# Preparing the key exponents of a gated-linear-attention chunk on GpSimd instead of VectorE, in a one-core Trainium2 transformer kernel

## The chip, the cores and the metric

The kernel runs on one core of a Trainium2 chip. The metric is the time of one execution in microseconds of device time; the figure given for a kernel is the median of its runs. Less is better. The engines are called TensorE (PE, with its weight loads PEld), VectorE (DVE), ScalarE (ACT), GpSimd (POOL) and SyncE (SP).

## What is computed

The reference is two transformer blocks over 512 tokens of width 1024 with a context of 256 tokens: a block with retention, window and neighbourhood attention and a mixture of experts, and then a second block of two layers. Each layer of the second block has three branches (latent attention, pooling, gated linear attention). The change touches only the gated linear attention (GLA), which is run forward and backward over chunks of 128 tokens:

```python
def gla_scan(q, k, v, log_a, s0, with_out):
    ...
    def step(s, inp):
        qq, kk, vv, aa = inp
        b = jnp.cumsum(aa, axis=2)
        b_last = b[:, :, -1:, :]
        s_new = jnp.exp(b_last)[:, :, 0, :, None] * s + jnp.einsum('bhcd,bhce->bhde', kk * jnp.exp(b_last - b), vv)
        inter = jnp.einsum('bhcd,bhde->bhce', qq * jnp.exp(b), s)
        decay = jnp.exp(jnp.where(mask, b[:, :, :, None, :] - b[:, :, None, :, :], -jnp.inf))
        attn = jnp.einsum('bhid,bhjd,bhijd->bhij', qq, kk, decay)
        intra = jnp.einsum('bhij,bhje->bhie', attn, vv)
        return s_new, inter + intra
```

There are 4 heads with 64 key and 128 value features. The kernel computes `attn` without the five-index product: it cuts the 128 queries of a chunk into 4 segments of 32, takes the running sum `b` in the middle of a segment as `mid`, and uses exp(b - mid) for queries and exp(mid - b) for keys, both exponents held at or below a clamp.

## The kernel before

All activations lie feature-major in on-chip memory: 128 features on the partitions, tokens along the free axis. Every engine has its own instruction stream, written by hand in program order inside `program`, and streams wait for one another on counted semaphores. `E.sig(name)` raises a semaphore when an instruction is done, `E.next(name)` waits for its next value, `E.own()` waits for the last one that the engine itself raised. There is no planner; the order of the text is the order of the work. Products go to PSUM in numbered groups that rotate over three slots: `E.written(group)` waits until TensorE has written one, `E.taken(group)` until it has been read.

Weights stream through a ring of SyncE transfers. Most weight tiles are split into a high part (ScalarE, `high`, L1235) and a low part (GpSimd, `low`, L2175), one op of 1024 elements per partition each, for a three-product matmul. `low(n)` in the GpSimd stream does the next n tiles. Both parts have two buffers.

A layer of the second block (`for l in LAYERS` in each stream) has, up to the change: modulation and norm; projections for GLA queries, keys, values and gates; the running sums `gB` (VectorE, L1991); exponents of the state keys (L2000 to L2005), their exponential (ScalarE, L1468), product with the keys (L2011), 24 transposes (L560); state products `U` (TensorE) with the state scan (L2019, L2022). Then comes the **chunk loop**. Layer 0 does all six chunks of 128 tokens (`OWN_CHUNKS`), layer 1 only the four of the image, 2 to 5. Chunk buffers are double (`gChunk(c % 2)`): QI, QS (512 elements per partition each), KS (2048: 2 directions, 2 tiles, 4 segments, 128 keys) and QZ (1024). They overlay the buffers that the transposes and state products read, `gT1` and `gKT`. For one chunk c:

- VectorE `chunk_exponents(c)`: QS = b - mid (L2035), KS = mid - b for two directions (L2040, 1024 elements each), then the minimum with the clamp for QS (L2044) and KS (L2045);
- ScalarE `chunk_exps(c)`: exponentials of QS (L1477), KS (L1479) and of b into QI (L1480);
- VectorE `chunk_products(c)`: per direction QI times queries (L2053), QS times queries into the two halves of QZ (L2056), KS times keys (L2061);
- TensorE: scores `A` (32 matmuls of 128x64), then, after VectorE, the output `Y` (16 matmuls of 128x128 when a chunk is the first of a direction's scan, 24 otherwise);
- VectorE: masks of the scores out of PSUM (L2080, four of 256 elements), and the sum of the directions (L2085, 512), which releases `Y`;
- ScalarE: evacuation of `Y` (L1492).

VectorE runs `chunk_products(c)`, `chunk_exponents(c + 1)`, masks and sum of c, in this order, with `chunk_exponents` of the first chunk ahead of the loop. ScalarE runs `chunk_exps(c + 1)` before the evacuation of c. GpSimd has `low(17)` ahead of and across the loop and nothing else until the stage ends. All matmuls of the helper `mm` carry line L557, all transposes L560.

Of the kernel before, what the change touches and what calls it, by code (L numbers as in the profile page):

```python
# [19 lines left out]
P = 128  # L20
# [4 lines left out]
TT = TOK // P  # L25
# [10 lines left out]
CLAMP = 1280.0  # L36
# [181 lines left out]
def program(nc, dram, scratch, out):  # L218
# [7 lines left out]
    with ExitStack() as ctx:  # L226
        def sbuf(name, cols):
            return ctx.enter_context(nc.sbuf_tensor(name, [P, cols], f32))
# [10 lines left out]
        parts = parts.rearrange("p (s x n) -> p s x n", s=2, x=2)  # L239
        split_tiles = [n for n, name in enumerate(plan) if is_split(name)]  # L240
        split_reader = []
        par = sbuf("params_sb", NPAR)
        con = sbuf("consts_sb", NCONST)
        with nc.sbuf_tensor("arena", [P, ARENA], f32) as arena:
# [299 lines left out]
        def _(pe):  # L544
# [505 lines left out]
            for l in LAYERS:  # L1050
# [51 lines left out]
                for c in OWN_CHUNKS[l]:  # L1102
                    QI, QS, KS, QZ = gChunk(c % 2)
                    pe.wait_ge(*E.next("chunk_operands"))
                    ps = group("A", l, c)
                    for d in range(2):
                        for t in range(2):
                            for s in range(4):

                                at = ((2 * d + t) * 4 + s) * 64  # L1110
                                ins = mm(ps[:, at:at + 64], KS[:, d, t, s, :],
                                         QZ[:, 2 * d + t, s, :, :].rearrange("p b n -> p (b n)"), True, True)
                    ins.then_inc(psum_full, 1)
                    pe.wait_ge(*E.next("chunk_weights"))
                    ps = group("Y", l, c)
                    for h in range(4):
                        hp = 64 * (h % 2)
                        terms = [(gV[:, c, h * P:(h + 1) * P], gAT[:, h * P:(h + 1) * P])]
                        for d in range(2):
                            if c != SCAN[d][0]:  # L1120
                                terms.append((gS[hp:hp + 64, d, c, h // 2, :],
                                              QI[hp:hp + 64, 2 * d + h // 2, :]))
                        for n, (a, b) in enumerate(terms):
                            at = (h % 2) * 512 + (h // 2) * P
                            ins = mm(ps[:, at:at + P], a, b, n == 0, n == len(terms) - 1)
                    ins.then_inc(psum_full, 1)
# [80 lines left out]
        def _(act):  # L1207
# [221 lines left out]
            for l in LAYERS:  # L1429
# [44 lines left out]
                def chunk_exps(c):  # L1474
                    QI, QS, KS, _ = gChunk(c % 2)
                    act.wait_ge(*E.next("chunk_exponents"))
                    act_(QS, QS, ACT.Exp, scale=1.0 / 16)  # L1477
                    ks = KS.rearrange("p d t s n -> p (d t s n)")
                    act_(ks, ks, ACT.Exp, scale=1.0 / 16)  # L1479
                    act_(QI, gB[:, :, c * P:(c + 1) * P], ACT.Exp, scale=1.0 / 16)\  # L1480
                        .then_inc(*E.sig("chunk_decays"))
# [85 lines left out]
        def _(dve):  # L1567
# [392 lines left out]
            for l in LAYERS:  # L1960
# [67 lines left out]
                def chunk_exponents(c):  # L2028

                    QI, QS, KS, _ = gChunk(c % 2)  # L2030
                    b = gB[:, :, c * P:(c + 1) * P]
                    b4 = b.rearrange("p a (s n) -> p a s n", s=4)
                    mid = b4[:, :, :, 15:16]
                    dve.wait_ge(*E.own())
                    tt_(QS.rearrange("p a (s n) -> p a s n", s=4), b4, mid.to_broadcast([P, 4, 4, 32]),  # L2035
                        ALU.subtract)
                    for d in range(2):
                        E_in = mid[:, 2 * d:2 * d + 2, :, :].to_broadcast([P, 2, 4, P])
                        E_b = b[:, 2 * d:2 * d + 2, :].unsqueeze(2).to_broadcast([P, 2, 4, P])
                        ins = tt_(KS[:, d, :, :, :], E_in, E_b, ALU.subtract)  # L2040
                    ins.then_inc(*E.sig("dve_step"))
                    dve.wait_ge(*E.own())
                    q, k = QS.rearrange("p a n -> p (a n)"), KS.rearrange("p d t s n -> p (d t s n)")
                    V.tensor_scalar_min(q, q, CLAMP)  # L2044
                    V.tensor_scalar_min(k, k, CLAMP).then_inc(*E.sig("chunk_exponents"))  # L2045

                def chunk_products(c):
                    QI, QS, KS, QZ = gChunk(c % 2)
# [111 lines left out]
        def _(pool):  # L2160
# [68 lines left out]
            for l in LAYERS:  # L2229
                if l == 0:  # L2230
                    pool.wait_ge(*E.next("ctx2_loaded", 16))
                    pool.wait_ge(*E.next("residual_ready", 3 * KT))
                else:
                    pool.wait_ge(*E.own())
                pool.dma_start(scratch, R3).then_inc(sem("residual_saved"), 16)
                low(17)

                pool.wait_ge(*E.own())
                G_.memset(tick[:, 2:3], 0.0).then_inc(*E.sig("pool_stage_done"))
                pool.wait_ge(*E.next("act_stage_done"))  # L2240
                pool.wait_ge(*E.next("dve_stage_done"))
                pool.dma_start(area(MW, 1024), dram["t_mla"]).then_inc(sem("mla_tables_loaded"), 16)
                low(1)

                pool.wait_ge(*E.own())
                G_.memset(tick[:, 2:3], 0.0).then_inc(*E.sig("pool_stage_done"))
                pool.wait_ge(*E.next("act_stage_done"))
                pool.wait_ge(*E.next("dve_stage_done"))
                pool.dma_start(pCnt, dram["t_count"]).then_inc(sem("counts_loaded"), 16)
                for b in range(2):  # L2250
                    for c0, n in ((0, 8), (264, 16), (792, 8)):
                        ins = G_.memset(pX[:, b * (TOK + 32) + c0:b * (TOK + 32) + c0 + n], 0.0)
                if l == 1:
                    for b in range(2):
                        ins = G_.memset(pX[:, b * (TOK + 32) + 8:b * (TOK + 32) + 264], 0.0)
                ins.then_inc(*E.sig("pads_zero"))
                pool.wait_ge(*E.next("pads_zero"))
                pool.wait_ge(*E.next("counts_loaded", 16))
                low(4)
                for g in range(4):  # L2260
                    low()
                    pool.wait_ge(*E.taken("px", l, g))
                    u = pX[:, (g % 2) * (TOK + 32):(g % 2 + 1) * (TOK + 32)]
                    a, w = u, TOK + 32

                    lo = 0
                    for n in range(g + 1):
                        o = pS[:, (n % 2) * w:(n % 2 + 1) * w]
                        s1 = 1 if n == 0 else 2 ** (n - 1)
                        s2 = 0 if n == 0 else 2 ** (n - 1)  # L2270
                        new = lo + s1
                        G_.tensor_tensor(o[:, new:w - new], a[:, new - s1:w - new - s1],  # L2272
                                                a[:, new + s2:w - new + s2], ALU.add).then_inc(*E.sig("pool_step"))
                        pool.wait_ge(*E.own())
                        a, lo = o, new
                    segs = ([(8, 0, CTX)] if l == 0 else []) + [(280, CTX, SEQ)]
                    for x0, c0, n in segs:
                        ins = G_.tensor_tensor(pO[:, g, c0:c0 + n], a[:, x0:x0 + n], pCnt[:, g, c0:c0 + n],
                                               ALU.mult)
                    ins.then_inc(*E.sig("pool_step"))  # L2280
                    pool.wait_ge(*E.own())
                    for x0, c0, n in segs:
                        ins = G_.tensor_tensor(pO[:, g, c0:c0 + n], pO[:, g, c0:c0 + n], u[:, x0:x0 + n],
                                               ALU.subtract)
                    ins.then_inc(*E.sig("pooled"))
                    low()
                low(24 + 4 * len(parted(("l", l))))

                pool.wait_ge(*E.written("gate", ("l", l), 2, KT - 1))
                pool.wait_ge(*E.next("residual_saved", 16))  # L2290
                pool.dma_start(R3, scratch).then_inc(sem("residual_reloaded"), 16)
                low(6)
                pool.wait_ge(sem("residual_reloaded"), 16 * (l + 2))
                for k in range(KT):
                    pool.wait_ge(*E.next("update_ready"))
                    v = slice(0, TOK) if l == 0 else slice(CTX, TOK)
                    G_.tensor_tensor(R3[:, k, v], R3[:, k, v], mOUT[:, k, v], ALU.add)\
                        .then_inc(*E.sig("residual_updated"))
# [96 lines left out]
```

## Time and profile before

| | us |
|---|---|
| median of 3 runs | 3560.37 |
| lowest, highest | 3553.74, 3569.28 |
| profiled execution | 3560.11 |
| its span in the trace | 3558.3 |
| mean granted TensorE clock | 0.92 |

The profiled execution lies 0.3 us from the median, and 1.8 us of it are outside the span. The chunk loop of layer 0 runs from about 1801.6 to 1912 us of the span, that of layer 1 from about 2893.7 to 2974; together they are some 190 us, 5% of the span. A row of the timeline gives start, duration, engine, line, operation, output and inputs, shape and count, and in brackets how long the engine had been idle and who ended that. Durations of one instruction include time in which it has been issued and is held up.

### The profile page before, as it was taken

What the parts mean: (1) busy time and instruction counts of PE and PEld (TensorE: products, weight loads), DVE (VectorE), ACT (ScalarE), POOL (GpSimd) and SP (SyncE); (2) the same over time, 40 slices, a digit from 0 to 9 for tenths busy, and PEclk for the clock granted to TensorE, in tenths of its full rate; (3) what the DMA queues carried; (4) which work ended last, traced back from release to release, by engine and by line L of the source; (5) the groups of instructions that cost most, each with busy time, mean ns of one, the idle gap of its engine ahead of it and who ended that gap; (6) DMA issues with size and microseconds to landing.
All of it is one profiled execution on the core that took longest, in us unless ns stands there. A gap on an engine that the chain in (4) does not pass through costs nothing.

```text
span 3558.3 us, 35935 instructions
## 1 busy us (share of the span) xinstructions
PE 3106.5 (87%) x14810; PEld 2247.3 (63%) x14810; DVE 1066.0 (30%) x1387; ACT 847.8 (24%) x1223; POOL 662.6 (19%) x348
## 2 busy tenths in 40 slices
PE   6889899999869999987769699999997948799996
PEld 1656787788633333324657378999993746387885
DVE  1235512411341111122266543111115075542112
ACT  0422322322300000013322233211123222233222
POOL 0221320044200000001200001522222201006443
PEclk9899999999879999998857899999998967899998
DMA  9011210022239999984100001111124100002221
GB/s 390 36 48 42 43 60 12 14 98 99 87 132 358 383 369 362 372 330 159 48 1 26 28 1 54 60 60 60 68 88 188 59 12 30 24 7 100 100 97 71
DMA packets 56488, 406.87 MB, mean 114 GB/s; under 512 B 6352, under 2 KB 6352, under 8 KB 9760
## 3 DMA queue, kind: packets, MB, share of 16 engines
q1 hardware_dynamic: 52416, 375.41, 27.8%
q0 software_dynamic: 3936, 29.48, 2.4%
q8 instruction: 105, 1.72, 0.2%
q14 instruction: 31, 0.25, 0.0%
HBM read 396.48 MB, written 8.39 MB: 114 GB/s over the span
## 4 chain that ended last, share of the span: by engine, by line
PE 77%; DVE 10%; DMA 6%; ACT 4%; issue 1%; POOL 1%; SPq 0%; DVEq 0%; POOLq 0%; ACTq 0%
PE psum L557 73%; DMA ring<-in_weights 6%; PE psum L560 3%; DVE arena L1583 1%; DVE arena L1614 1%; DVE arena L1613 1%; ACT hidden_high L1256 1%; ACT hidden L1250 1%; DVE arena L1617 1%; POOL arena L2272 0%; DVE arena L2155 0%; DVE arena L1991 0%; DVE arena L2080 0%; DVE arena L2094 0%; ACT weight_parts L1235 0%
## 5 line engine op out<-in xcount | busy, mean ns | idle before, releaser
L557 PE MATMUL psum<-hidden_high,weight_parts 128*128 128x384 f32 (+1 forms) x3296 | 866.8, 364 | 56.2 <-DVE hidden_low L1596 41.8
L2175 POOL TENSOR_TENSOR weight_parts<-ring,weight_parts 128x1024 fp32r<-128x1024 f32 x218 | 532.1, 2442 | 1693.6 <-ACT weight_parts L1235 1688.2
L557 PE MATMUL psum<-arena 128*128 128x64 f32 (+8 forms) x2992 | 651.8, 372 | 92.7 <-DVE arena L2061 32.4
L557 PEld LDWEIGHTS psum<-hidden_high,weight_parts 128*128 128x128 f32 x3296 | 609.4, 191 | 132.5 <-issue 51.7
L557 PEld LDWEIGHTS psum<-arena 128*128 128x128 f32 (+3 forms) x2992 | 435.7, 214 | 249.9 <-issue 213.5
L557 PE MATMUL psum<-hidden_low,weight_parts 128*128 128x384 f32 (+1 forms) x1648 | 518.4, 362 | 0.0
L1235 ACT ACTIVATE weight_parts<-ring 128x1024 fp32r<-128x1024 f32 x218 | 231.0, 1061 | 1141.0 <-PE psum L557 1123.9
L557 PE MATMUL psum<-ring,arena 128*64 128x512 f32 (+1 forms) x1560 | 380.3, 604 | 44.5 <-DMA ring<-in_weights 39.3
L557 PE MATMUL psum<-arena_parts,weight_parts 128*128 128x512 f32 (+1 forms) x1728 | 368.5, 373 | 12.9 <-DVE arena_parts L1717 12.9
L557 PEld LDWEIGHTS psum<-arena_parts,weight_parts 128*128 128x128 f32 x1728 | 317.9, 190 | 58.4 <-issue 14.3
L1265 ACT ACTIVATE arena<-psum 128x512 f32<-128x512 f32 (+4 forms) x234 | 165.9, 713 | 696.5 <-PE psum L557 457.3
L557 PEld LDWEIGHTS psum<-hidden_low,weight_parts 128*128 128x128 f32 x1648 | 309.1, 192 | 26.6 <-issue 0.5
L557 PEld LDWEIGHTS psum<-ring,arena 128*64 128x64 f32 (+1 forms) x1560 | 105.5, 137 | 267.9 <-issue 162.8
L1704 DVE TENSOR_TENSOR arena<-arena,psum 128x512 f32<-128x512 f32 (+1 forms) x72 | 55.9, 777 | 595.1 <-PE psum L557 595.1
L1637 DVE TENSOR_REDUCE small<-psum 128x1 f32<-128x768 f32 (+3 forms) x144 | 122.9, 854 | 333.8 <-PE psum L557 333.8
L560 PE MATMUL psum<-consts_sb,arena 128*128 128x128 f32 x968 | 145.5, 286 | 64.3 <-DVE arena L2011 45.4
L557 PE MATMUL psum<-arena,consts_sb 128*128 128x512 f32 (+3 forms) x362 | 166.7, 596 | 29.5 <-DVE arena L1613 15.5
L560 PEld LDWEIGHTS psum<-consts_sb,arena 128*128 128x128 f32 x968 | 120.8, 149 | 87.9 <-DVE arena L2011 46.1
L1287 ACT ACTIVATE arena<-psum,small 128x768 f32<-128x768 f32 (+3 forms) x144 | 117.3, 815 | 225.1 <-DVE small L1637 222.9
L557 PE MATMUL psum<-arena,ring 128*128 128x384 f32 (+5 forms) x344 | 124.7, 529 | 31.0 <-DVE arena L2116 21.2
L557 PE MATMUL psum<-weight_parts,hidden_high 128*128 128x512 f32 (+1 forms) x480 | 139.2, 375 | 10.9 <-issue 8.8
L557 PEld LDWEIGHTS psum<-arena,consts_sb 128*128 128x128 f32 (+2 forms) x362 | 70.1, 201 | 110.8 <-issue 63.8
(224 smaller groups left out, 2039.1 us busy)
## 6 DMA issues: line engine op xcount, KB each, us to landing
ring<-in_weights SPq DMA_DIRECT2D x356, 1024.0 KB, 5.0
saved_residual<-residual POOLq DMA_DIRECT2D x2, 3072.0 KB, 14.3
residual<-saved_residual POOLq DMA_DIRECT2D x2, 3072.0 KB, 11.2
arena<-in_rpb POOLq DMA_DIRECT2D x16, 224.0 KB, 8.2
residual<-in_acts POOLq DMA_DIRECT2D x1, 3072.0 KB, 19.3
arena<-in_t_count POOLq DMA_DIRECT2D x2, 1536.0 KB, 7.4
residual<-in_acts POOLq DMA_DIRECT2D x1, 2048.0 KB, 11.0
out_x<-residual SPq DMA_DIRECT2D x8, 256.0 KB, 2.0
```

Of the source, the lines that this page charges most:

```text
L557: return nc.tensor.matmul(o, lhsT, rhs, start=start, stop=stop)
L560: return nc.tensor.transpose(o, a, C("ident")[0:a.shape[0], 0:a.shape[0]])
L1235: act_(parts[:, i % 2, 0, :], ring[:, at:at + 1024], ACT.Copy).then_inc(*E.sig("high_written"))
L1250: ins = act_(H3[:, k, CTX:TOK], H3[:, k, CTX:TOK], ACT.Identity, bias=mod[:, col + k, 0:1])
L1256: act_(Hhi[:, k, :], H3[:, k, :], ACT.Copy).then_inc(*E.sig("hidden_high"))
L1265: act_(dst, src, func, **kw).then_inc(*E.read(*name))
L1287: act_(pP[:, i % 2, 0:L + CTX], ps[:, 512 - L:768], ACT.Exp, bias=negmax[:, col:col + 1], accum_out=sums[:, col:col + 1]).then_inc(*E.read ...
L1583: V.reciprocal(r, r).then_inc(*E.sig("dve_step"))
L1613: tt_(tmp, ps[p0:p1, 0:SEQ], sin, ALU.mult).then_inc(*E.read("rot", *name))
L1637: ins = V.reduce_max(nm, ps[:, 512 - L:768], AXX, negate=True)
L1704: tt_(to, tok_view(mSG[:, gate_slot(f, b, g), :], chunks), bank_view(ps, chunks), ALU.mult).then_inc(*E.read("branch", key, b, g))
L2175: G_.tensor_tensor(parts[:, i % 2, 1, :], ring[:, at:at + 1024], parts[:, i % 2, 0, :], ALU.subtract).then_inc(*E.sig("tile_split"))
```

## The change

The key exponents (two subtractions and the minimum on KS) leave VectorE's `chunk_exponents` and are issued by GpSimd in a loop of its own over the layer's chunks. That loop stands after 12 of the 17 tile splits; the other 5 follow it. GpSimd first waits for both `decayed_keys` signals; for the first two chunks of a layer it then waits for the last state products of both directions to be written, and for every later chunk c until the scores of chunk c - 2 are written (`chunk_sums` records that group count in TensorE's stream). ScalarE waits for the new signal `key_chunk_exponents` between the exponential of QS and that of KS.

```diff
@@ TensorE, chunk loop, after the scores
                     ins.then_inc(psum_full, 1)
+                    chunk_sums.append(state["g"])
                     pe.wait_ge(*E.next("chunk_weights"))
@@ ScalarE, chunk_exps
                     act.wait_ge(*E.next("chunk_exponents"))
                     act_(QS, QS, ACT.Exp, scale=1.0 / 16)
+                    act.wait_ge(*E.next("key_chunk_exponents"))
                     ks = KS.rearrange("p d t s n -> p (d t s n)")
@@ VectorE, chunk_exponents
                     tt_(QS.rearrange("p a (s n) -> p a s n", s=4), b4, mid.to_broadcast([P, 4, 4, 32]),
-                        ALU.subtract)
-                    for d in range(2):
-                        E_in = mid[:, 2 * d:2 * d + 2, :, :].to_broadcast([P, 2, 4, P])
-                        E_b = b[:, 2 * d:2 * d + 2, :].unsqueeze(2).to_broadcast([P, 2, 4, P])
-                        ins = tt_(KS[:, d, :, :, :], E_in, E_b, ALU.subtract)
-                    ins.then_inc(*E.sig("dve_step"))
+                        ALU.subtract).then_inc(*E.sig("dve_step"))
                     dve.wait_ge(*E.own())
-                    q, k = QS.rearrange("p a n -> p (a n)"), KS.rearrange("p d t s n -> p (d t s n)")
-                    V.tensor_scalar_min(q, q, CLAMP)
-                    V.tensor_scalar_min(k, k, CLAMP).then_inc(*E.sig("chunk_exponents"))
+                    q = QS.rearrange("p a n -> p (a n)")
+                    V.tensor_scalar_min(q, q, CLAMP).then_inc(*E.sig("chunk_exponents"))
@@ GpSimd, layer of the second block
                 pool.dma_start(scratch, R3).then_inc(sem("residual_saved"), 16)
-                low(17)
+                low(12)
+                pool.wait_ge(*E.next("decayed_keys", 2))
+                for c in OWN_CHUNKS[l]:
+                    KS = gChunk(c % 2)[2]
+                    b = gB[:, :, c * P:(c + 1) * P]
+                    mid = b.rearrange("p a (s n) -> p a s n", s=4)[:, :, :, 15:16]
+                    n = (c if l == 0 else TT + c - 2) - 2
+                    if c >= OWN_CHUNKS[l][0] + 2:
+                        pool.wait_ge(psum_full, chunk_sums[n])
+                    else:
+                        for d in range(2):
+                            pool.wait_ge(*E.written("U", l, d, SCAN[d][-2]))
+                    for d in range(2):
+                        E_in = mid[:, 2 * d:2 * d + 2, :, :].to_broadcast([P, 2, 4, P])
+                        E_b = b[:, 2 * d:2 * d + 2, :].unsqueeze(2).to_broadcast([P, 2, 4, P])
+                        G_.tensor_tensor(KS[:, d, :, :, :], E_in, E_b, ALU.subtract).then_inc(*E.sig("pool_step"))
+                    pool.wait_ge(*E.own())
+                    k = KS.rearrange("p d t s n -> p (d t s n)")
+                    G_.tensor_scalar_min(k, k, CLAMP).then_inc(*E.sig("key_chunk_exponents"))
+                low(5)
```

## Rows read from the trace of the kernel before

**Rows 1.** The page: busy time by engine, and the chain that ended last.
```profile
PE 3106.5 (87%) x14810; PEld 2247.3 (63%) x14810; DVE 1066.0 (30%) x1387; ACT 847.8 (24%) x1223; POOL 662.6 (19%) x348
PE 77%; DVE 10%; DMA 6%; ACT 4%; issue 1%; POOL 1%; SPq 0%; DVEq 0%; POOLq 0%; ACTq 0%
```

**Rows 2.** Windows of layer 0's loop: length; busy PE, PEld, DVE, ACT, POOL; PEclk; DMA.
```profile
1798.00:1814.00 16.00, 0.03 (x2) 0.00 (x0) 12.28 (x20) 2.95 (x3) 0.00 (x0) 0.63 0.00 0
1822.00:1837.00 15.00, 12.87 (x48) 10.89 (x48) 11.17 (x19) 3.55 (x4) 0.00 (x0) 0.50 0.00 1
...
1852.00:1870.00 18.00, 14.58 (x56) 12.60 (x56) 12.46 (x22) 3.55 (x4) 0.00 (x0) 0.50 0.00 1
```

**Rows 3.** Chain that ended last, 1750 to 1900: start us, us, what.
```profile
1774.50 3.66 issue
...
1805.04 1.15 DVE arena L2045
...
1812.73 1.24 DVE arena L2061
...
1821.38 1.43 DVE arena L2080 x4
...
1822.83 0.70 DVE arena L2085
```

**Rows 4.** Timeline of VectorE, one turn of the loop.
```profile
1823.63 0.43 DVE L2053 TENSOR_TENSOR arena<-arena 128x256 f32<-128x256 f32 x1
...
1828.43 0.69 DVE L2035 TENSOR_TENSOR arena<-arena 128x512 f32<-128x512 f32 x1
...
1836.56 1.42 DVE L2080 TENSOR_TENSOR arena<-psum,consts_sb 128x256 f32<-128x256 f32 x4 [3.57 <-PE psum L557]
```

**Rows 5.** Timeline of TensorE: state products, first scores, last output product.
```profile
1795.79 2.24 PE L557 MATMUL psum<-arena 128*64 128x128 f32 x30
1814.21 7.06 PE L557 MATMUL psum<-arena 128*128 128x64 f32 x32 [16.18 <-DVE arena L2061]
...
1904.59 7.57 PE L557 MATMUL psum<-arena 128*128 128x128 f32 x24 [2.30 <-DVE arena L2085]
```

**Rows 6.** Groups by shape, VectorE, whole span: the removed subtractions.
```profile
L2040 DVE TENSOR_TENSOR arena<-arena 128x1024 f32<-128x1024 f32 x20 | 23.5, 1218 | 0.0
```

**Rows 7.** Groups by shape, GpSimd, whole span (busy us, mean ns | idle before).
```profile
L2199 POOL TENSOR_TENSOR arena<-arena 128x896 f32<-128x896 f32 x8 | 16.4, 2086 | 11.0 <-DMA arena<-in_rpb 11.0
...
L2272 POOL TENSOR_TENSOR arena<-arena 128x798 f32<-128x798 f32 x8 | 12.1, 1517 | 0.0
L2278 POOL TENSOR_TENSOR arena<-arena 128x512 f32<-128x512 f32 x8 | 10.3, 1288 | 0.3
...
L2278 POOL TENSOR_TENSOR arena<-arena 128x256 f32<-128x256 f32 x4 | 2.9, 735 | 0.3
...
L2207 POOL MEMSET arena<- 64x2048 f32 x1 | 1.8, 1807 | 69.4 <-DVE small L1829 69.4
```

**Rows 8.** Timelines of VectorE and GpSimd where they meet: 176, 1769 and 3542 us.
```profile
175.91 0.69 DVE L1613 TENSOR_TENSOR arena<-psum,arena 128x512 f32<-128x512 f32 x1 [53.29 <-PE psum L557]
176.51 2.57 DVE L1614 TENSOR_TENSOR arena<-arena 128x512 f32<-128x512 f32 x1
...
176.19 2.35 POOL L2175 TENSOR_TENSOR weight_parts<-ring,weight_parts 128x1024 fp32r<-128x1024 f32 x1 [5.92 <-ACT weight_parts L1235]
...
1770.64 3.78 DVE L2002 TENSOR_TENSOR arena<-arena 128x1536 f32<-128x1536 f32 x1
...
1778.16 1.75 DVE L2005 TENSOR_TENSOR arena<-arena 128x1536 f32<-128x1536 f32 x1
...
1769.77 6.85 POOL L2175 TENSOR_TENSOR weight_parts<-ring,weight_parts 128x1024 fp32r<-128x1024 f32 x2 [26.37 <-ACT weight_parts L1235]
...
3542.12 11.42 DVE L2155 SCALAR_TENSOR_TENSOR arena<-arena,small 128x512 f32<-128x512 f32 x8
3543.01 12.87 POOL L2297 TENSOR_TENSOR residual<-residual,arena 128x512 f32<-128x512 f32 x8 [23.36 <-DVE arena L2155]
```

More of the change, by code:

```diff
@@ L241, in program @@
         split_reader = []
+        chunk_sums = []
         par = sbuf("params_sb", NPAR)
```

## The prediction

> **What bounds the kernel now.** I read the page first: TensorE is busy 87% of the span and makes up 77% of the chain that ended last, GpSimd is busy 19% [rows 1]. That is an average over many stages, so the chunk loops have to be read by themselves. The windows view cuts the first layer's loop into stretches: GpSimd does nothing there at all, VectorE is busy 11 to 12 us of each 15 to 18, and TensorE's granted clock is 0.50, the lower of its two levels (1.2 GHz), through the whole loop, after 16 us in which it had done almost nothing [rows 2]. Further waiting of TensorE can therefore not lower the clock there.
>
> The chain of waits tells who sets the pace [rows 3]. Before the first scores VectorE and ScalarE are on it: exponents, exponentials, products. From the first scores on, the chain is a ring of three: TensorE's block, four masks (L2080, 1.43 us), one add (L2085, 0.70 us), TensorE again. VectorE's other work for a chunk is off the chain. Its timeline shows how far off [rows 4]: after the add come the products of the next chunk (L2053, L2056, L2061; 1823.63 to 1828.4, so 4.8 us), then the exponents of the chunk after it (L2035, L2040, L2044, L2045; 4.6 us), then it idles 3.57 us until the next scores. TensorE's block is the output product of this chunk plus the scores of the next: 12.87 us for 48 matmuls in the early chunks, 14.58 us for 56 later [rows 2]; the scores alone are 7.06 us and the longer output product alone 7.57 [rows 5]. So the output product takes 12.87 - 7.06 = 5.8 us at first and 7.5 later, and the next scores need the products that long after the add: the products' 4.8 us are hidden with **1.0 us** to spare in the early chunks and 2.8 us in the later ones. That margin, not VectorE's idle time, is what the change can break.
>
> **What is removed.** Ten times (six chunks, then four) VectorE no longer does two subtractions of 1.22 us [rows 6] and a minimum of 1.2 us [rows 3], 3.6 us a chunk. For eight chunks they lie under TensorE's block and return nothing. For the first chunk of each layer they are on the chain [rows 3], so at most 2 x 3.6 = 7 us, 0.2%, can be won by them.
>
> **What is added.** GpSimd does the same three, on 1024, 1024 and 2048 elements per partition. Its rows [rows 7]: a two-input op takes 2.09 us for 896 elements, 1.52 for 798, 1.29 for 512 and 0.735 for 256; a fill of 2048 takes 1.81. A tile split of 1024 takes 2.35 [rows 8]. I take 2.2 to 2.4 us for each subtraction. No row has a one-input op. Below it is the fill, which reads nothing (1.8 us); above it the two-input rate, (1288 - 735) / 256 = 2.16 ns an element, 4.4 us. Reading one operand instead of two is half of the latter, so I take 2.2 us, about 6.7 us of GpSimd a chunk. GpSimd has the time: it does nothing in the loop now [rows 2]. By the Trainium skill (GPSIMD Engine Reference, section 3.1) a good one-input loop there runs at about 1.8 cycles an element at 1.2 GHz; by that, as an estimate, the minimum is 3.1 us and the sum below would be 7 us larger. No row here shows it.
>
> The splitting of weight tiles is cut in two, 12 tiles and then 5. So the 13th split moves from ahead of the loop, where it is the second of the two at 1769.77 [rows 8], to behind GpSimd's last chunk. It is first read after the loop, more than a period later, so nobody waits for it; what it disturbs is priced below. No DMA is moved: the save of the residual stands before both parts. ScalarE's new wait stands after the query exponential, with the key and query-decay exponentials and the evacuation of the previous output queued behind it; in mid-loop the keys come 8 us after the scores and ScalarE reaches the wait some 13 us after them, so it is free.
>
> **Where it collides.** The trace of before has the experiment in it [rows 8]. At 176 us a VectorE op reading PSUM and SBUF takes its normal 0.69 us beside a GpSimd op; the one behind it, with both inputs in SBUF, takes 2.57 instead of 0.68 and ends 0.54 us after the GpSimd op does. At 1769 us two tile splits meet three equal VectorE ops: the two caught take 3.78 us each (one is shown) where a free one takes 1.75, and the two GpSimd ops take 6.85 instead of 4.7. At 3542 us eight of each take turns strictly: 13.8 us for both, or 1.7 a pair. So they exclude each other instruction by instruction and alternate when both are queued; one GpSimd op of 1024 then holds VectorE about 2.2 us. Now the products and the add L2085 read two SBUF operands; the masks L2080 read PSUM and are safe.
>
> The change starts GpSimd on chunk c exactly when the scores of chunk c-2 are done, which is also what releases VectorE's masks. Call that T, and walk it:
> - first subtraction T+0.1 to T+2.4; masks run free to T+1.5; the add waits and ends at T+3.0 instead of T+2.2. This is **0.8 us** on the chain by itself;
> - second subtraction to T+5.2; the first product (L2053) waits for it, ends T+5.5;
> - minimum T+5.5 to T+7.7, with the next product waiting;
> - the other products need their 4.4 us and end at T+12.1; the scores start 0.24 us later [rows 3, 5] at T+12.35, end T+19.4.
> Before, the period was 2.3 + 5.8 + 7.06 = 15.2 us early and 16.9 later. It becomes 19.4: **+4.2** or **+2.5**. It happens for every chunk whose c-2 was scored in the same layer: four in the first layer (two early, two late periods), two in the second (late): 2 x 4.2 + 4 x 2.5 = 18.4 us.
>
> The 13th split: ahead of the loop it no longer delays L2004, which is on the chain (the 3.66 us called issue in [rows 3] are L2004's own): 3.78 - 1.75 = 2.0 us won in each layer. It now follows the last minimum at once and holds VectorE's products once more, about T+8.0 to T+10.2: 2.2 us lost in each layer. Net +0.4 us.
>
> The start of a layer: GpSimd may begin once the last state product is written, 1798.0 (1795.79 + 2.24, [rows 5]). In the times of before, two subtractions end at 1802.8; VectorE's query subtraction, ready at 1801.6, ends 1803.3; the minimum ends 1805.5 and ScalarE is done at 1808.9, against 1809.17 before. But GpSimd goes on at once with the second chunk: 1805.8 to 1808.0 to 1810.2, one product, minimum to 1812.7, the other products to 1817.1. The scores start at 1817.35, not 1814.21: +3.1 us. The second layer has the same pattern, so 6.3 us. **Sum: 18.4 + 0.4 + 6.3 = +25 us.** The profiled execution took 3560.1 us (span 3558.3), 0.3 us from the median of the three runs, so 3585 us on either.
>
> Ends for the unknown durations: with subtractions at the 798-element row's rate (1.8 us held) and the minimum at the fill's 1.7, the same walk gives +3.0 and +1.3 a period and +0.6 a start, +12 us (3572). With the minimum at 4.4 us every one of six periods and two starts gains 2.2: +42 us (3602).
>
> **Rivals.**
> - *The minimum does not block.* Rows show exclusion only against GpSimd ops with two inputs. Then products end at T+9.9: +2.0 in two early periods, +0.8 in four late ones, +0.2 a start: +8 us, 3568, within noise. The Trainium skill (SBUF — State Buffer, "Who interferes with whom") says that any GpSimd op that reads SBUF excludes VectorE ops with two SBUF inputs; by that rule this rival is out, and no row here decides it.
> - *No collision in the loop (not slower).* If the small VectorE ops slip in between, or GpSimd's broadcast reads leave VectorE alone, masks, add and products keep their 2.2 and 4.8 us. Then only the start counts: keys at 1805.2, ScalarE done at 1807.6, 1.5 us earlier than before, and the split ahead of the loop gives its 2.0: twice 3.5, so -7 us, 3553. It decides from the point where the products still fit under 5.8 us. For it: every colliding row is of ops of 512 elements or more, the products are of 256 and 1024. Against: [rows 8] show no exception for two-SBUF-input ops that start behind a GpSimd op.
> - *GpSimd is slower than its rows.* Its operands are repeated along an axis and strided; at 3 us a subtraction and 4.4 for the minimum the sum goes to +50 us, 3610. Against: the row of 896 elements also has a repeated operand and costs 2.09.
>
> **How the numbers follow.** The collision in full has 0.66 (own range 3572 to 3602), the harmless minimum 0.10, no collision 0.08, a slower GpSimd 0.16. The forecast is the first, 3585 us. The range 3564 to 3606 holds the first two cases and the near part of the last. A measurement can tell about 0.5%, 18 us, from no change: slower by more than that needs 3578. Most of the first case (about 0.8 of it) and the last lie above: 0.68. Faster by 0.5% is out of reach of all that can be won (7 us at the starts, 4 from the split), and is left 0.03. The rest, 0.29, is no change.
>
> **What would show it.** In the profile after: L2085 at 1.4 to 1.5 us instead of 0.69 in six chunks; a product op behind each GpSimd op at 2 us or more; TensorE waiting for L2061 in mid-loop, which it does not now; GpSimd's minimum near 2.2 us; periods of 19 us. In the last two chunks of each layer the old times return. If L2085 stays at 0.69 the mechanism is wrong; if it grows and the period doesn't, the margin was.

## The result and the profile after

The changed kernel takes 3600.82 us, the median of 8 runs (3585.04 to 3603.61), against 3563.3 us for the kernel before in its 8 (3553.74 to 3570.16). The ratio is 1.0087, with a 95% interval of 1.0072 to 1.0102, so the change costs between 26 and 36 us. The two medians lie further apart, 37.5 us or a ratio of 1.0105. The change makes the kernel slower, as forecast. The median lies inside the stated range (3564 to 3606) but near its upper end, and the forecast of +25 us (1.0070) lies just below the interval of the ratio.

The page of the kernel after, the two lines that answer to [rows 1]:

```profile
PE 3111.7 (86%) x14810; PEld 2247.7 (62%) x14810; DVE 1082.2 (30%) x1357; ACT 847.0 (24%) x1223; POOL 754.9 (21%) x378
PE 75%; DVE 12%; DMA 7%; ACT 4%; POOL 1%; issue 1%; SPq 0%; DVEq 0%; POOLq 0%; ACTq 0%
```

VectorE issues 30 instructions fewer and yet is busy 16 us longer (1066.0 before): the time that it no longer computes it now spends, and more, being held up inside other instructions. Its part of the chain rises from 10% to 12%.

**Where the time is.** The profiled execution took 3601.9 us (span 3600.1), 41.8 us more than that of before by the spans. I cut both traces at the same instructions: the subtraction ahead of the running sums (L1986 before, L1989 after), the first fill at the loop (L2065, L2062) and the first norm row after it (L2089, L2086).

| stretch, us | before | after | difference |
|---|---|---|---|
| start to layer 0's subtraction | 1757.4 | 1771.0 | +13.6 |
| layer 0: subtraction to fill | 42.1 | 39.8 | -2.3 |
| layer 0: fill to norm (the loop) | 117.2 | 139.1 | +21.9 |
| between the layers' stretches | 932.8 | 931.5 | -1.3 |
| layer 1: subtraction to fill | 42.1 | 39.4 | -2.8 |
| layer 1: fill to norm | 85.8 | 99.0 | +13.2 |
| layer 1's norm to the end | 580.9 | 580.4 | -0.5 |

The four stretches that the change touches give **+30.0 us**, near the middle of the ratio's interval. The 13.6 us ahead of them are not the change's: nothing there was edited, and in the executions of the experiments below the same stretch took anything from 1755.9 to 1779.0 us, whatever the kernel (1755.9 in experiment 3, whose text up to there is that of the change). What makes it vary no run tells. So I read every experiment by these four stretches, which I call **the layers**: 287.3 us before, 317.2 after.

GpSimd's groups by shape, after (busy us, mean ns of one | idle before):

```profile
L2251 POOL TENSOR_SCALAR arena<-arena 128x2048 f32<-128x2048 f32 x10 | 54.6, 5462 | 0.9
L2248 POOL TENSOR_TENSOR arena<-arena 128x1024 f32<-128x1024 f32 x20 | 40.6, 2051 | 105.0 <-PE psum L558 104.8
```

The minimum takes 5.4 us, not 2.2, and lies outside my upper bound of 4.4. That is not only how its row is drawn: at the start of the layer the minimum begins at 1813.32 and GpSimd's next op at 1819.08. A subtraction takes 1.91 us where nothing delays it, not 2.3.

One turn of the loop after, to be held against [rows 4] and [rows 5]: VectorE, then GpSimd, then TensorE.

```profile
1838.39 1.42 DVE L2077 TENSOR_TENSOR arena<-psum,consts_sb 128x256 f32<-128x256 f32 x4 [6.24 <-PE psum L558]
1839.84 0.99 DVE L2082 TENSOR_TENSOR arena<-arena 128x512 f32<-128x512 f32 x1
1840.93 1.95 DVE L2050 TENSOR_TENSOR arena<-arena 128x256 f32<-128x256 f32 x1
1842.80 4.28 DVE L2053 TENSOR_TENSOR arena<-arena 64x256 f32<-64x256 f32 x2
1847.09 1.22 DVE L2058 TENSOR_TENSOR arena<-arena 128x1024 f32<-128x1024 f32 x1
...
1838.37 4.23 POOL L2248 TENSOR_TENSOR arena<-arena 128x1024 f32<-128x1024 f32 x2 [9.96 <-PE psum L558]
1842.69 5.41 POOL L2251 TENSOR_SCALAR arena<-arena 128x2048 f32<-128x2048 f32 x1
...
1840.88 5.86 PE L558 MATMUL psum<-arena 128*128 128x128 f32 x16 [2.60 <-DVE arena L2082]
1850.71 7.09 PE L558 MATMUL psum<-arena 128*128 128x64 f32 x32 [3.97 <-DVE arena L2058]
```

GpSimd's ops begin with VectorE's masks. The masks (L2077) still take 1.42 us. The add (L2082) has grown from 0.69 to 0.99, the first product from 0.43 to 1.95, the first pair of half products from 0.85 to 4.28. The block of 12.87 us that TensorE ran without a break is now split, with 3.97 us of waiting for the products (L2058) between output and scores. The chain of waits shows the same thing as a new member of the ring; its entries from 1838 on:

```profile
1839.84 1.00 DVE arena L2082
...
1840.93 1.95 DVE arena L2050
1842.88 3.76 DVE arena L2053
...
1850.71 7.10 PE psum L558 x32
```

The output product is off the chain, the next chunk's products are on it. A period, from the masks of one chunk to those of the next, is 19.5 us where it was 15.2 or 16.9, and 21.7 for the one in each layer that the split of tile 13 falls into. The last period of each layer, with no keys left to prepare, is 16.9 as before. The granted clock is 0.50 throughout the loop, as before, so the longer waits cost no clock there.

### The profile page after: what moved, and what is told of

Its sections match the earlier page's. It is cut to its first block, busy times and chain, and to the rows that moved or that the text cites. A ratio compares the mean times of both kernels' runs of the same rounds, so it can differ in the third digit from the quotient of the medians.

```text
span 3600.1 us, 35939 instructions
## 1 busy us (share of the span) xinstructions
PE 3111.7 (86%) x14810; PEld 2247.7 (62%) x14810; DVE 1082.2 (30%) x1357; ACT 847.0 (24%) x1223; POOL 754.9 (21%) x378
## 4 chain that ended last, share of the span: by engine, by line
PE 75%; DVE 12%; DMA 7%; ACT 4%; POOL 1%; issue 1%; SPq 0%; DVEq 0%; POOLq 0%; ACTq 0%
PE psum L558 71%; DMA ring<-in_weights 7%; PE psum L561 3%; DVE arena L1586 1%; DVE arena L2053 1%; DVE arena L1617 1%; DVE arena L1616 1%; DVE arena L2050 1%; ACT hidden_high L1258 1%; ACT hidden L1252 1%; DVE arena L1620 1%; DVE arena L2058 1%; POOL arena L2288 0%; DVE arena L2152 0%; DVE arena L1994 0%
## 5 line engine op out<-in xcount | busy, mean ns | idle before, releaser
L1289 ACT ACTIVATE arena<-psum,small 128x768 f32<-128x768 f32 (+3 forms) x144 | 117.2, 814 | 227.5 <-DVE small L1640 227.4
L558 PE MATMUL psum<-ring,small 128*2 128x512 f32 x384 | 97.6, 639 | 50.8 <-DMA ring<-in_weights 43.0
## 6 DMA issues: line engine op xcount, KB each, us to landing
saved_residual<-residual POOLq DMA_DIRECT2D x2, 3072.0 KB, 14.7
```

Of the source, the lines that this page charges most:

```text
L558: return nc.tensor.matmul(o, lhsT, rhs, start=start, stop=stop)
L1289: act_(pP[:, i % 2, 0:L + CTX], ps[:, 512 - L:768], ACT.Exp, bias=negmax[:, col:col + 1], accum_out=sums[:, col:col + 1]).then_inc(*E.read ...
```

## The experiments

Seven kernels, each shown as edits against the changed kernel; a line without a sign tells in words what an engine does. Theory: VectorE's ops with two SBUF inputs and GpSimd's ops exclude each other, and GpSimd's three fall on the only place where VectorE has 1 us to spare. Rivals: the hand-over between engines costs, or GpSimd's keys are simply late.

**1. Signals without work** (one execution)

```diff
 VectorE: key subtractions and minimum as before
-                    for d in range(2):
-                        ...
-                        G_.tensor_tensor(KS[:, d, :, :, :], E_in, E_b, ALU.subtract).then_inc(*E.sig("pool_step"))
                     pool.wait_ge(*E.own())
-                    G_.tensor_scalar_min(k, k, CLAMP).then_inc(*E.sig("key_chunk_exponents"))
+                    G_.memset(tick[:, 2:3], 0.0).then_inc(*E.sig("key_chunk_exponents"))
```

> VectorE does the key exponents itself again; GpSimd keeps all its new waits and its signal, but a one-element fill stands in for its three ops, and the split of tile 13 stays behind them. Theory (the ops exclude VectorE's two-SBUF-input ops, the signals cost nothing): the add after the masks is back at 0.69 us in all but one chunk of each layer (the one that tile 13's split meets, about 1 us), periods are 15.2 and 16.9 us, and layer starts are as before; from the exponent subtraction to the loop about 2 us less than before in each layer. Both layers together 2 to 4 us faster than before. Rival (the hand-over costs: ScalarE waits for another engine and everything queued behind it comes late): periods stay near 19.5 us and the layers lose 15 us or more against before.

The layers took 283.8 us, 3.4 less than before. Periods are 15.18 and 16.88, but 17.65 where tile 13's split starts with the masks. VectorE and GpSimd there:

```profile
1869.26 1.41 DVE L2083 TENSOR_TENSOR arena<-psum,consts_sb 128x256 f32<-128x256 f32 x4 [5.29 <-PE psum L558]
1870.71 1.46 DVE L2088 TENSOR_TENSOR arena<-arena 128x512 f32<-128x512 f32 x1
...
1869.27 2.35 POOL L2178 TENSOR_TENSOR weight_parts<-ring,weight_parts 128x1024 fp32r<-128x1024 f32 x1
```

The add ends 0.55 us after the split does, about its own length of 0.69: it ran only when the split was nearly done. The 3.4 us are those of tile 13, whose split no longer meets the exponents ahead of the loop (4.9 us in both layers together) and costs 0.8 us a layer where it meets the add. All of the change's waits and signals together cost nothing that shows; the ops cost it.

**2. The same ops, later** (timed in 3 rounds)

```diff
+                    if c > OWN_CHUNKS[l][0]:
+                        pool.wait_ge(*E.upto("chunk_operands", n + 2))
                     if c >= OWN_CHUNKS[l][0] + 2:
                         pool.wait_ge(psum_full, chunk_sums[n])
```

> The change with one wait more: from a layer's second chunk on GpSimd also waits until VectorE has finished the products of the chunk before, so the same three ops run in VectorE's free time. Theory (what costs is whom they meet): GpSimd's keys come 5 to 10 us later than in the change, and it is faster all the same. Add at 0.69 us, products 4.8 us, TensorE's wait for products in mid-loop at most 2.5 us in the early chunks and near 0 later; the first scores come 1.9 us later than before instead of 5.8. Layers: 4 us over before (0 to 8), where the change is 30 over. Rival (what costs is GpSimd's longer time from scores to keys): slower than the change, by 5 us a chunk.

The layers took 291.9 us: +4.6 over before instead of +30.0, with every GpSimd op of the change still there and every key from the second chunk on later against the scores. The ratio to before is 1.0004 (0.9992 to 1.0017). The turn that answers to the one above, GpSimd's rows last:

```profile
1838.35 0.69 DVE L2082 TENSOR_TENSOR arena<-arena 128x512 f32<-128x512 f32 x1
1841.96 0.42 DVE L2050 TENSOR_TENSOR arena<-arena 128x256 f32<-128x256 f32 x1 [2.91 <-ACT arena L1483]
...
1829.56 4.46 POOL L2250 TENSOR_TENSOR arena<-arena 128x1024 f32<-128x1024 f32 x2 [8.15 <-DVE arena L2058]
1834.11 5.36 POOL L2253 TENSOR_SCALAR arena<-arena 128x2048 f32<-128x2048 f32 x1
```

Add and product are at their old lengths; what remains is that ScalarE now waits for the keys and VectorE 2.91 us for ScalarE. Periods are 17.1 to 17.25. For TensorE's wait I had expected near 0 in the late chunks and at most 2.5 in the early ones; the periods grew by 0.4 and 2. Each layer's first scores come 1.9 us later after the first fill than before, as expected. There were two explanations, whom the ops meet and how late the keys come, and this decides between them: lateness is the small part.

**3. Tile 13 ahead of the loop again** (one execution)

```diff
-                low(12)
+                low(13)
...
-                low(5)
+                low(4)
```

> The change with the split of tile 13 ahead of the key exponents again, as before. Theory: the stretch from the exponent subtraction to the loop is back at 42.1 us in both layers (39.8 and 39.4 in the change), and the one period of 21.7 us in each layer becomes 19.5. Both cancel: the layers within 1 us of the change. Rival (the 21.7 us period is of the last keys themselves): it stays 21.7, and the layers lose 4 us more.

Subtraction to fill is 41.9 and 42.1 us, the long period is 19.51 like the others, the layers 317.8 us against 317.2. The split of one weight tile costs 2.3 to 2.8 us a layer where it meets the exponents and 2.15 where it meets the products. So the long period is the split's and not that of the last keys, and the prediction's account of the 13th split holds.

**4. The minimum on VectorE** (timed in 3 rounds)

```diff
-                    V.tensor_scalar_min(q, q, CLAMP).then_inc(*E.sig("chunk_exponents"))
+                    V.tensor_scalar_min(q, q, CLAMP)
+                    dve.wait_ge(*E.next("key_differences", 2))
+                    k = KS.rearrange("p d t s n -> p (d t s n)")
+                    V.tensor_scalar_min(k, k, CLAMP).then_inc(*E.sig("chunk_exponents"))
 GpSimd:
-                    pool.wait_ge(*E.own())
-                    G_.tensor_scalar_min(k, k, CLAMP).then_inc(*E.sig("key_chunk_exponents"))
```

> GpSimd does only the two subtractions, VectorE the minimum again. Theory: GpSimd excludes VectorE for 3.8 us a chunk instead of about 7.5. The add stays at 0.99 us, the first product at about 1.95 us, the second product is back at 0.42 instead of 3.84. Products end about 9 us after the scores: periods 16.2 us early and 17.2 later, layer starts within 2 us of before. Layers +3 to +8 us over before, where the change has +30. Rival (each hand-over between the engines costs a fixed time, whatever the length of the op): two of three ops are left, so two thirds of the loss, about +20.

GpSimd's two subtractions raise `key_differences` in place of `pool_step`, and ScalarE's wait for `key_chunk_exponents` is gone, which the excerpt does not show.

The layers took 289.2 us, +2.0: below the 3 to 8 expected. The ratio is 1.0004 (0.9988 to 1.0020). Early periods are 16.08. One turn of VectorE:

```profile
1825.22 0.98 DVE L2084 TENSOR_TENSOR arena<-arena 128x512 f32<-128x512 f32 x1
1826.31 1.95 DVE L2052 TENSOR_TENSOR arena<-arena 128x256 f32<-128x256 f32 x1
1828.17 0.84 DVE L2055 TENSOR_TENSOR arena<-arena 64x256 f32<-64x256 f32 x2
```

Add and first product are held as in the change, the half products are not. Taking the minimum back to VectorE removes 28 of the 30 us. The 2 us left are a balance: with the subtractions alone the periods of both layers are 5.1 us longer than before (0.9 for an early one) and the first scores come 1.3 us later in each layer, against 5.7 us gained ahead of the fills, where tile 13 is no longer split.

**5. A fill in place of the minimum** (one execution)

```diff
-                    G_.tensor_scalar_min(k, k, CLAMP).then_inc(*E.sig("key_chunk_exponents"))
+                    G_.memset(k, 0.0).then_inc(*E.sig("key_chunk_exponents"))
```

> The change with a fill of the same 2048 elements in place of GpSimd's minimum; it overwrites the differences, so the keys' decay within a chunk is left out of this kernel's output. Question: does GpSimd's third op hold VectorE back because it reads, or because GpSimd is busy? Theory (only a reading op excludes an op with two SBUF inputs): the fill takes about 1.8 us, and the second product (64x256) is back at 0.42 us although it meets the fill; the first product still waits for the second subtraction (1.95 us). Periods 16.1 early and 17.2 late, the layers about 2 us over before. Rival (any GpSimd op excludes it for its whole length): the second product takes about 1.8 us, periods 17.5 to 18, the layers +10 to +13 us over before.

VectorE and GpSimd where the fill meets the half products, and then where it meets the clamp of the queries at the start of the layer:

```profile
1838.02 1.95 DVE L2050 TENSOR_TENSOR arena<-arena 128x256 f32<-128x256 f32 x1
1839.89 0.84 DVE L2053 TENSOR_TENSOR arena<-arena 64x256 f32<-64x256 f32 x2
...
1839.74 1.80 POOL L2251 MEMSET arena<- 128x2048 f32 x1
...
1818.24 1.56 DVE L2042 TENSOR_SCALAR arena<-arena 128x512 f32<-128x512 f32 x1
...
1817.72 1.80 POOL L2251 MEMSET arena<- 128x2048 f32 x1
```

The half products run at 0.84 for the two beside a fill that began before them: an op that only writes does not hold back ops with two SBUF inputs. The clamp (L2042, one input, 512 elements in 0.43 us when free, where the add of as many with two inputs takes 0.69) does wait for the fill's end, 1.56 us. The periods are 16.08 early and 17.18 late (18.2 with tile 13's split), as the theory had them, not the 17.5 to 18 of the rival.

The layers took 284.2 us, 3.1 under before; I had expected 2 over, since I had left out that the start of a layer gets shorter too, by 1.6 us. GpSimd's three ops for the first chunk take longer than VectorE's took, but they begin 1.3 us ahead of the first fill and end 4.3 us after its start, where VectorE's minimum ended 6.65 us after it.

**6. An addition in place of the minimum** (one execution)

```diff
-                    G_.tensor_scalar_min(k, k, CLAMP).then_inc(*E.sig("key_chunk_exponents"))
+                    G_.tensor_tensor(k, k, tick[:, 8:9].to_broadcast([P, 2048]), ALU.add)\
+                        .then_inc(*E.sig("key_chunk_exponents"))
```

> The change with GpSimd's minimum replaced by an addition of a zero column (two inputs); the clamp on the key exponents is left out. Question: is the 3.84 us of the second product the length of GpSimd's op, or only its reading part? The minimum's row says 5.41 us, but the product behind it ended 1.45 us before that row's end. Theory (a two-input op costs 1.9 ns an element and blocks until its end): the row reads 3.9 us, shorter than the one-input minimum, while the second product still takes about 3.8 to 4.0 us, so the periods stay at 19.4 to 19.7 us; only the layer starts shorten, by 1.5 us each or more, because ScalarE gets the first keys earlier. Rival (the product's wait is a fixed share of the row, 0.7 of it): the second product falls to 2.8 us and the periods to 18.4.

`tick[:, 8:9]` is a column that GpSimd fills with zeros once, far ahead of the layers.

```profile
1849.25 4.25 DVE L2053 TENSOR_TENSOR arena<-arena 64x256 f32<-64x256 f32 x2
...
1849.12 3.66 POOL L2253 TENSOR_TENSOR arena<-arena,small 128x2048 f32<-128x2048 f32 x1
```

GpSimd's row is 1.75 us shorter than the minimum's, the two half products take 4.25 us, as behind the minimum (4.28 in the change), and the periods are 19.48. The minimum therefore holds such an op for about 3.5 us of its 5.41, and the last part of its row holds it no more; the addition holds it to its end. The layers took 313.3 us, 3.9 less than with the change; 3.6 of that are the two layer starts.

**7. Only what is on the chain, and early** (timed in 5 rounds)

```diff
 GpSimd:
+                pool.wait_ge(*E.written("KT", l, 1, 2))
-                for c in OWN_CHUNKS[l]:
+                for c in OWN_CHUNKS[l][:1]:
...
+                pool.wait_ge(*E.next("chunk_operands", len(OWN_CHUNKS[l])))
                 low(5)
 VectorE: key subtractions and minimum as before for all but the first chunk
 ScalarE:
-                    act.wait_ge(*E.next("key_chunk_exponents"))
+                    if c == OWN_CHUNKS[l][0]:
+                        act.wait_ge(*E.next("key_chunk_exponents"))
```

> GpSimd prepares the key exponents of a layer's first chunk alone, as soon as the key transposes are written (they no longer need the buffer) and ahead of the state scan's end; VectorE does all later chunks as before; tiles 13 to 17 are split once the last chunk's products are done. Theory: both things that were on the chain are hidden: 3.4 us at the start of a layer (keys ready before VectorE's fills end; first scores 1.2 + 2 x 1.2 us earlier) and 2.0 us of the tile split that met the exponent subtractions. Periods 15.2 and 16.9 us and every add at 0.69 us, as before. Layers 11 us faster than before (8 to 12), total about 3555 against 3566, ratio 0.997. Rival (GpSimd's early ops meet the state scan, whose ops read PSUM and one or two small SBUF operands): the scan's 0.34 us ops get longer and up to 5 us a layer are given back.

The waits of GpSimd's loop on the state products and on `chunk_sums` are gone too; the wait on the key transposes (`KT`) stands in their place.

This kernel is **faster than both**: 3555.71 us against 3569.68 for the kernel before on the same chip, ratio 0.9963 (0.9948 to 0.9977). The layers took 275.0 us, 12.3 under before, slightly more than the 8 to 12 expected: 5.5 of them come ahead of the fills, from the split of tile 13 alone, and 6.8 from the two layer starts. GpSimd's ops lie beside the state scan:

```profile
1800.31 2.53 DVE L2026 SCALAR_TENSOR_TENSOR arena<-arena,small,psum 128x128 f32<-128x128 f32 x8
...
1808.23 0.69 DVE L2039 TENSOR_TENSOR arena<-arena 128x512 f32<-128x512 f32 x1
...
1798.26 3.79 POOL L2253 TENSOR_TENSOR arena<-arena 128x1024 f32<-128x1024 f32 x2 [16.06 <-PE psum L561]
1802.14 5.36 POOL L2256 TENSOR_SCALAR arena<-arena 128x2048 f32<-128x2048 f32 x1
1895.85 2.34 POOL L2182 TENSOR_TENSOR weight_parts<-ring,weight_parts 128x1024 fp32r<-128x1024 f32 x1 [88.34 <-DVE arena L2068]
```

The scan's ops, which read PSUM, keep their 2.53 us for eight, so the rival is out. The first scores start 11.3 us after the first fill instead of 14.7.

## Why the prediction was right, and where it was off

*What bounds the kernel.* Right. The margin of 1.0 us between the products and the end of the output product was the thing that broke; VectorE's idle time of 3.57 us grew to 6.2 and bought nothing.

*Where it collides.* Right in kind, in place and in order: masks free, add held, first product behind the second subtraction, half product behind the minimum. Experiments 1, 2, 4 and 5 show it from four sides. The Trainium skill's rule (SBUF — State Buffer, "Who interferes with whom"), that a GpSimd op which reads SBUF excludes VectorE ops with two SBUF inputs while one that only writes does not, is what the minimum and the fill did. The rival built on a harmless minimum is out, and so is that of no collision. That of a GpSimd slower than its rows was half true: the minimum, at 5.4 us, is slower than even this rival's 4.4, but the subtractions, at 1.91, are faster than the 2.2 to 2.4 that I took.

*What it costs in mid-loop.* The period came out right by luck, because two terms were wrong against each other. From the end of the scores (T, about 1838.3):

| | forecast | measured |
|---|---|---|
| add ends | T+3.0 | T+2.5 |
| first product ends | T+5.5 | T+4.6 |
| half product behind the minimum ends | T+8.1 | T+8.3 |
| next scores start | T+12.35 | T+12.4 |
| period, early and late | 19.4, 19.4 | 19.5, 19.5 |

The subtractions were 0.4 us shorter each than I had taken, which brought the end of the first product forward by 0.9 us; the step behind the minimum took 3.7 us (T+4.6 to T+8.3) where I had 2.6, 1.1 more. The add took 0.99 us, below the 1.4 to 1.5 that I had named as a sign. The six periods gave 23.5 us, of which 4.3 are tile 13's: 19.2 against 18.4.

*The start of a layer.* **The term that failed.** I had +3.1 us a layer; first fill to first scores takes 20.5 us where it took 14.7, +5.8. The minimum stands twice on that path and there the shorter subtractions do not make up for it. The first time its whole length counts and not only the 3.5 us for which it holds a product, since ScalarE needs the finished keys: it ends 8.2 us after the start of the first fill, where my walk had 6.0. The clamp of the queries, which ScalarE needs as well, is not released early as the two-input ops are and ends 0.3 us after it:

```profile
1813.81 5.47 DVE L2042 TENSOR_SCALAR arena<-arena 128x512 f32<-128x512 f32 x1
...
1813.32 5.67 POOL L2251 TENSOR_SCALAR arena<-arena 128x2048 f32<-128x2048 f32 x1
```

ScalarE is done 2.1 us later after the fill than in my walk, and from there to the scores, with the second minimum on the way, it is 0.5 us more. Two layers: 11.6 against 6.3 us. These 5.3 us are all of the missing 5.

*Tile 13.* Right: -5.1 ahead of the loops (I had -4.0) and +4.3 in them (+4.4).

*The price of the minimum.* My value was half of the two-input rate, on the argument that one operand is read instead of two. Experiment 6 shows the argument false: on 2048 elements the two-input addition takes 3.66 us and the one-input minimum 5.41. The row that I took as an upper bound was none, since it is another operation. The Trainium skill (GPSIMD Engine Reference, section 3.1) gives 1.8 cycles an element as the best case of a tight loop, not as the rate of this instruction; the 3.1 us that I worked out from it as an estimate were too low as well. By the 1.2 GHz that the Trainium skill gives there, the measured 5.41 us are 3.2 cycles an element.

In sum: 19.2 + 11.6 + 4.3 - 5.1 = 30.0 us against 25. The median of 3600.82 us lies 15.8 us above the forecast of 3585; the terms above account for 5 of them. The rest lies outside the layers, as the 13.6 us ahead of layer 0's subtraction do in the profiled execution, and its cause is open.

Two side sums of the prediction are off as well, without effect on the forecast: the terms of the low end (3.0 and 1.3 a period, 0.6 a start, 0.4 for the split) add up to 12.8 us and not 12, and the terms of a slower GpSimd to about 54 and not 50.

## What to carry to other kernels

Before work goes from VectorE to GpSimd, list which VectorE instructions will run beside it and how many inputs they have in SBUF: here those with an operand in PSUM kept their time (four masks 1.42 us, eight ops of the scan 2.53) and so did VectorE's fills (0.91 beside a subtraction), while those with two inputs in SBUF and the clamp took turns with it. A freed engine gains nothing if the instruction that is now late is the next one on the chain. The same three ops cost 15 us a layer when released by the event that also releases VectorE's urgent work, and about 2 when released after it. With only the first chunk moved, and put beside work that reads PSUM, they gained 3.4 us a layer. And move first what is on the chain: here that was the first chunk of each layer, two in ten, and one weight split a layer.

## What the hardware showed that I had not expected

- A one-input op with a constant on GpSimd (minimum, float32, 128x2048) takes 5.41 us, a two-input one of the same size 3.66 (an addition), a fill 1.80. Only the minimum was tried; what makes it slow no run tells.
- The reach of an exclusion depends on both ops. GpSimd's minimum held a VectorE op with two SBUF inputs for about 3.5 us of its 5.41, but the one-input clamp (0.43 us for 512 elements when free) until the end; a fill held the first kind not at all and the second to its end.
- GpSimd's two-input rate is not one number: 1.91 us for 1024 elements here (a subtraction), 2.34 to 2.40 for a tile split of the same size, whose output is of another type (fp32r). No run tells whether that is the cause.
